# Identity products where TensorE waits, and a reordered router and transition, in a two-block model kernel

## Chip, cores and metric

The kernel runs on one NeuronCore of a Trainium2 chip. The metric is the device time of one execution in microseconds (us); before the change the median of three runs is 1951.22 us (1948.08 to 1958.10).

## What is computed

Two transformer blocks over 256 tokens of width 1024, in float32. The first mixes an mLSTM and a sparse attention under a modulation computed from `c`, and ends in a mixture of 32 experts; the second has two layers of attention, a recurrent branch and a feed-forward part. What the change touches, cut from the reference:

```python
mod = jnp.dot(jax.nn.silu(c), w_ada[l]) + b_ada[l]            # 1024 x 6144, in six parts
sh1, sc1, gt1, sh2, sc2, gt2 = [m[:, None, :] for m in jnp.split(mod, 6, axis=-1)]
h = rmsnorm(x, g_pre_mix[l]) * (1.0 + sc1) + sh1
...
h2 = rmsnorm(x, g_pre_ffn[l]) * (1.0 + sc2) + sh2
logits = jnp.dot(xf, w_router) + b_router                     # 32 experts
vals, idx = lax.top_k(logits, 4)
gate = jax.nn.softmax(vals, axis=-1)
...                                                           # each picked (token, expert) pair is evaluated
up = jnp.dot(xb, w_up[eb]) + b_up[eb]
glu, lin = jnp.split(up, 2, axis=-1)
act = jnp.minimum(glu, 7.) * jax.nn.sigmoid(1.702 * jnp.minimum(glu, 7.)) * (jnp.clip(lin, -7., 7.) + 1.0)
y = jnp.dot(act, w_down[eb]) + b_down[eb]
...
x = x + gt2 * rmsnorm(y2, g_post_ffn[l])                      # the hand-over to the second block
```

## The kernel before

The program is written by hand: one instruction stream for each engine, ordered by semaphores. Each engine works strictly in the order of its stream; TensorE's weight loads may run ahead of its products. Eight PSUM banks `pb[0..7]` of 128 x 512 float32 are assigned by hand.

*Modulation.* The first third of `w_ada`, as far as shift and scale of the first mix need it, comes in eight row slabs of 1 MB. `modulation(k)` (L1130, products at L1135) multiplies slab k with a column of `silu(c)`, four products of 512 columns into four strips of bank 6. After slab 6 two transposes turn the parameter rows (L1175, L1176); after slab 7 VectorE copies the bank (L809), `first_columns` (L1143) turns the row into columns, VectorE makes shift and scale (L814, L815) and h, one chunk at a time (L817). Then come the gate rows (`rows`, L1199: h against 32 gate columns), the flips of the attention bias (L1209, products with a flipped identity into banks 5, 6, 7, 3), a ScalarE and VectorE chain over the gates (L605 to L848), and the column units of `w_in` (L1191), which load slab by slab as earlier slabs are used up.

*Router.* The last output slab's columns are gained and turned (L1451) and `route` (L1459) adds up the logits in bank 7. VectorE makes X1 and later the top four of each token (L1042 to L1059), ScalarE its squares (L754) and the scaled rows h2 (L760). TensorE turns X1 into columns (L1488), then waits for `logits_ready` and makes the places of the picked pairs (L1493 to L1497: counts with the strict lower triangle `before` and with ones, for two token tiles). VectorE turns places into a selection (L1068 to L1071), TensorE gathers the rows of the first expert (`gather`, L1574), ScalarE copies them (L768), TensorE turns them (`turn_rows`, L1581, into bank 0) and ScalarE makes scaled columns of them (`expert_columns`, L567).

*Experts.* `tensor_pass` runs 34 passes of 64 rows: `up` (bias products L1603, then eight weight chunks L1612), `gather` of the next pass, `scatter` of the last pass (L1591, into banks 4 to 7), transposes (L1618, L1624), `down` (L1633). Pass 0 stands outside the loop and has some router work between its halves (`halfway`). Each expert's 12 slabs of 1 MB come as six double slabs through three double places, the anteroom; GpSimd copies them into the ring (L1553) when the slab's place is used up (`expert_used`), and SyncE issues the next double slab into the freed place (`sync_experts`, L1536 and L1540). The first three of expert 1 wait for h2 and the turned X1.

*Transition.* When the last scatter is done (`acc_done`), ScalarE squares the four result banks 4 to 7 (L2147) and loads the square root's table (L2148); VectorE scales the banks by `gt2` (L2322); TensorE sums the eight squared chunks over partitions (L1864); ScalarE takes the root (L2144), VectorE its reciprocal (L2324), the scaled parts (L2331) and the new x (L2328); ScalarE's scaled x (L2154) feeds the second block's first products (L1900). GpSimd's loads of the second block wait for the first square.

## Time and profile before

| | |
|---|---|
| median of 3 runs | 1951.22 us (1948.08 to 1958.10) |
| profiled execution | 1952.78 us, its span 1951.0 us |
| mean granted TensorE clock | 0.985 |
| TensorE busy | 1896.1 us, 97% of the span |
| GpSimd, VectorE, ScalarE busy | 706.7, 610.5, 410.1 us |
| chain that ended last | TensorE 84%, DMA 8%, VectorE 3% |
| DMA | 553.49 MB, mean 284 GB/s |

The profile is of one execution. Busy times are of instructions, not of waits; PE is TensorE, PEld its weight loads, DVE VectorE, ACT ScalarE, POOL GpSimd, SP SyncE.
### The profile page before, as it was taken

What the parts mean: (1) busy time and instruction counts of PE and PEld (TensorE: products, weight loads), DVE (VectorE), ACT (ScalarE), POOL (GpSimd) and SP (SyncE); (2) the same over time, 40 slices, a digit from 0 to 9 for tenths busy, and PEclk for the clock granted to TensorE, in tenths of its full rate; (3) what the DMA queues carried; (4) which work ended last, traced back from release to release, by engine and by line L of the source; (5) the groups of instructions that cost most, each with busy time, mean ns of one, the idle gap of its engine ahead of it and who ended that gap; (6) DMA issues with size and microseconds to landing.
All of it is one profiled execution on the core that took longest, in us unless ns stands there. A gap on an engine that the chain in (4) does not pass through costs nothing.

```text
span 1951.0 us, 25907 instructions
## 1 busy us (share of the span) xinstructions
PE 1896.1 (97%) x9600; PEld 1148.8 (59%) x9601; DVE 610.5 (31%) x1304; ACT 410.1 (21%) x981; POOL 706.7 (36%) x406
## 2 busy tenths in 40 slices
PE   7999999999999999999999998999999999999999
PEld 4886733333333333333333335877888888788887
DVE  1756422322332232223331333664010126521000
ACT  2134322212221222212211222351000003500000
POOL 0000057777777777777767772000000000000000
PEclk8999989999999999999999999999999999999999
DMA  9873889999999999999999999243434652344330
GB/s 353 269 251 120 314 335 425 427 427 424 429 426 388 427 426 425 428 425 426 427 395 428 426 425 324 92 130 129 130 105 110 185 190 85 114 140 146 96 104 22
DMA packets 194760, 553.49 MB, mean 284 GB/s; under 512 B 13387, under 2 KB 151006, under 8 KB 160910
## 3 DMA queue, kind: packets, MB, share of 16 engines
q1 hardware_dynamic: 189872, 549.45, 73.0%
q10 hardware_dynamic: 4270, 1.98, 0.4%
q0 software_dynamic: 560, 1.25, 0.3%
q8 instruction: 41, 0.67, 0.1%
q14 instruction: 17, 0.14, 0.0%
HBM read 551.59 MB, written 1.06 MB: 283 GB/s over the span
## 4 chain that ended last, share of the span: by engine, by line
PE 84%; DMA 8%; DVE 3%; issue 2%; POOL 2%; ACT 1%; SPq 0%; POOLq 0%; ACTq 0%; DVEq 0%
PE bank L1612 19%; PE bank L1885 18%; PE bank L1633 10%; PE bank L2118 8%; DMA ring_and_columns<-in_w_up_dram 7%; PE bank L1890 4%; PE bank L1191 3%; PE bank L1591 3%; PE bank L1574 3%; PE bank L1900 2%; PE bank L1199 2%; PE bank L1472 2%; POOL ring_and_columns L1553 2%; PE bank L2004 1%; PE bank L1603 1%
## 5 line engine op out<-in xcount | busy, mean ns | idle before, releaser
L1553 POOL COPY ring_and_columns<-ring_and_columns 128x2048 f32<-128x2048 f32 x248 | 463.1, 1898 | 244.3 <-PE bank L1612 107.2
L1612 PE MATMUL bank<-ring_and_columns,cst 128*64 128x512 f32 x2176 | 480.3, 597 | 8.2 <-POOL ring_and_columns L1553 8.2
L1612 PEld LDWEIGHTS bank<-ring_and_columns,cst 128*64 128x64 f32 x2176 | 151.7, 137 | 334.4 <-issue 289.5
L1885 PE MATMUL bank<-ring_and_columns 128*128 128x272 f32 (+1 forms) x1536 | 342.7, 386 | 0.0
L1885 PEld LDWEIGHTS bank<-ring_and_columns 128*128 128x128 f32 x1536 | 291.8, 190 | 49.9
L1553 POOL COPY ring_and_columns<-anteroom_last 128x2048 f32<-128x2048 f32 x124 | 231.5, 1897 | 68.7 <-DMA anteroom_last<-in_w_up_dram 30.2
L1633 PE MATMUL bank<-ring_and_columns,pass_work 128*64 128x512 f32 x1088 | 242.5, 598 | 5.4 <-DVE pass_work L1735 5.4
L1633 PEld LDWEIGHTS bank<-ring_and_columns,pass_work 128*64 128x64 f32 x1088 | 77.9, 137 | 148.2 <-issue 144.0
L2118 PE MATMUL bank<-ffn_act,ring_and_columns 128*128 128x272 f32 (+1 forms) x704 | 157.1, 386 | 0.0
L2118 PEld LDWEIGHTS bank<-ffn_act,ring_and_columns 128*128 128x128 f32 x704 | 133.7, 190 | 22.8
L1726 DVE TENSOR_SCALAR pass_work<-bank 128x512 f32<-128x512 f32 x34 | 23.5, 692 | 338.7 <-PE bank L1612 338.7
L1686 ACT ACTIVATE pass_work<-pass_work 128x512 f32<-128x512 f32 x34 | 21.4, 630 | 470.8 <-DVE pass_work L1726 470.8
L567 ACT ACTIVATE cst<-bank,expert_affine_by_pair 128x64 f32<-128x64 f32 x280 | 86.9, 417 | 88.2 <-PE bank L1581 88.2
L1711 DVE COPY hot<-cst 64x64 f32 x34 | 31.8, 936 | 231.0 <-PE bank L1603 231.0
L2548 DVE TENSOR_TENSOR probs<-bank,probs 128x272 f32<-128x272 f32 (+1 forms) x40 | 15.4, 427 | 251.5 <-ACT probs L2304 251.5
L1890 PE MATMUL bank<-ring_and_columns 128*128 128x256 f32 x384 | 85.5, 381 | 0.0
L1890 PEld LDWEIGHTS bank<-ring_and_columns 128*128 128x128 f32 x384 | 72.2, 190 | 11.5 <-issue 2.0
L1191 PE MATMUL bank<-ring_and_columns 128*128 128x256 f32 x320 | 70.6, 380 | 0.0
L2304 ACT ACTIVATE probs<-bank 128x272 f32<-128x272 f32 (+1 forms) x40 | 13.4, 388 | 269.6 <-PE bank L1885 269.6
L1591 PEld LDWEIGHTS bank<-cst,pass_work 64*128 64x128 f32 x544 | 49.7, 186 | 32.9 <-issue 26.8
L1574 PE MATMUL bank<-h_rows_sb,psel 128*64 128x512 f32 x280 | 67.6, 604 | 1.1 <-DVE psel L1071 1.1
L1591 PE MATMUL bank<-cst,pass_work 64*128 64x256 f32 x544 | 67.9, 389 | 0.7 <-ACT pass_work L1693 0.7
(506 smaller groups left out, 1718.3 us busy)
## 6 DMA issues: line engine op xcount, KB each, us to landing
ring_and_columns<-in_w_up_dram SPq DMA_DIRECT2D x97, 2048.0 KB, 10.6
ring_and_columns<-in_w_down_dram SPq DMA_DIRECT2D x33, 2048.0 KB, 10.6
anteroom_last<-in_w_up_dram SPq DMA_DIRECT2D x31, 2048.0 KB, 10.5
anteroom_last<-in_w_down_dram SPq DMA_DIRECT2D x31, 2048.0 KB, 10.7
ring_and_columns<-in_w_gu_dram SPq DMA_DIRECT2D x44, 1024.0 KB, 5.4
ring_and_columns<-in_w_in_dram SPq DMA_DIRECT2D x33, 1024.0 KB, 10.4
ring_and_columns<-in_w_down_dram SPq DMA_DIRECT2D x32, 704.0 KB, 6.1
ring_and_columns<-in_w_ada_dram SPq DMA_DIRECT2D x8, 2048.0 KB, 12.3
```

The lines of the kernel that those rows point to most:

```text
L567: ins = act.activation(xe[:, k, :], turned[:, k % (WIDE // P), k // (WIDE // P), :], ACT.Identity, bias=PAB[:, 0, k:k + 1], scale=PAB[:, 1 ...
L1191: ins = mm(dst, w(k), hv[:, k, :], start=(k == 0), stop=(k == CHUNKS - 1))
L1199: ins = mm(dst, hv[:, k, P * t:P * t + P], w(k), start=(k == 0), stop=(k == CHUNKS - 1))
L1472: ins = mm(y_bank(j, t)[:, y_at(j, t)], yv[:, k, P * t:P * t + P], w[:, k, :], start=(k == 0), stop=(k == CHUNKS - 1))
L1553: pool.tensor_copy(ring[:, k, :], anteroom(j % ANTE)[:, SLOT * half:SLOT * half + SLOT]).then_inc(ante_copied, 1)
L1574: ins = mm(bankG[CAP * g:CAP * g + CAP, 0:WIDE], psel[:, t, :], h2[:, t, WIDE * g:WIDE * g + WIDE], start=(t == 0), stop=(t == 1))
L1591: ins = mm(pb[4 + (WIDE // P * g + k) // 2][:, S * (k % 2):S * (k % 2) + S], ye[r, P * k:P * k + P], pgt[r, :], start=False, stop=False, s ...
L1612: ins = mm(bank[CAP * g:CAP * g + CAP, 0:WIDE], xe[:, k, :], ring[:, k, a:a + WIDE], start=False, stop=(k == CHUNKS - 1))
L1633: ins = mm(bankY[CAP * g:CAP * g + CAP, 0:WIDE], rows_, w[:, WIDE * g:WIDE * g + WIDE], start=(k == 0), stop=(k == CHUNKS - 1))
L1885: ins = mm(bank[:, 0:columns], w[:, k, P * m:P * m + P], src[:, k, 0:columns], start=(k == 0), stop=(k == CHUNKS - 1))
L1890: ins = mm(pb[bank][:, a:a + 256], hT[:, k, P * t:P * t + P], w[:, k, :], start=(k == 0), stop=(k == CHUNKS - 1))
L2118: ins = mm(pb[DOWN_BANKS[l][m]][:, 0:n], w[:, k, :], FA[:, kk, 0:n], start=(kk == 0), stop=(kk == NF - 1))
```

## The change

A helper `keep_busy(bank, n)` issues n products of the identity with the 256 constant columns that begin with the identity, into a bank that is unused there. It is called in the modulation (three ahead of slabs 5 and 6, two ahead of slab 7, two behind it, two behind the column products) and in the router (two ahead of the transposes of X1, two ahead of the wait for the logits, two behind the placement). The placement products become three with wider operands. VectorE's subtraction for the gates' exponential moves behind the mask that TensorE waits for. The first pass's turned rows go to bank 2 instead of bank 0, and `up` waits for its columns behind the bias products (pass 0) or behind the first half of them (later passes). In the transition the last scatter signals twice, the squares run in the order of banks 4, 6, 5, 7, VectorE adds the two halves of each squared bank so that TensorE sums four chunks instead of eight, and the scaling by `gt2` is merged into the scaling by the reciprocal.

```diff
-        def expert_columns(act):
-            turned = pb[0][:, 0:WIDE].rearrange("p (c g n) -> p c g n", c=WIDE // P, g=GROUPS)
+        def expert_columns(act, bank):
+            turned = bank[:, 0:WIDE].rearrange("p (c g n) -> p c g n", c=WIDE // P, g=GROUPS)
...
-            tt(RW[:, 3, :, :], LG[:], spread_last(V8[:, :, 0], E), ALU.subtract).then_inc(s["logit_exp_in"], 1)
             tt(RW[:, 0, :, :], LG[:], v4, ALU.is_gt)
...
             dve.sem_inc(s["logits_ready"], 1)
+            tt(RW[:, 3, :, :], LG[:], spread_last(V8[:, :, 0], E), ALU.subtract).then_inc(s["logit_exp_in"], 1)
...
+            def keep_busy(bank, n):
+                both = cst[:, cat["ident"][0]:cat["ident"][0] + S]
+                for _ in range(n):
+                    mm(bank[:, 0:S], ident, both, start=True, stop=True)
...
+            pe.wait_ge(s["trel_copied"], 1)
             for k in range(FIRST_CHUNKS, CHUNKS - 1):
+                if k >= 5:
+                    keep_busy(pb[7], 3)
                 modulation(k)
...
+            keep_busy(pb[7], 2)
             modulation(CHUNKS - 1)
+            keep_busy(pb[7], 2)
             pe.wait_ge(s["const_ready"], 7)
             pe.wait_ge(s["params_ready"], 1)
             first_columns()
+            keep_busy(pb[7], 2)
...
             route(3).then_inc(s["routed"], 1)
+            keep_busy(pb[3], 2)
             for b in range(4):
...
+            keep_busy(pb[3], 2)
             pe.wait_ge(s["logits_ready"], 1)
-            m0, m1 = RW[:, 5, 0, :], RW[:, 5, 1, :]
-            mm(pb[7][:, 0:E], C["before"], m0, start=True, stop=True)
-            mm(pb[7][:, E:2 * E], ones[:], m0, start=True, stop=False)
-            mm(pb[7][:, E:2 * E], C["before"], m1, start=False, stop=True)
-            mm(pb[7][:, 2 * E:3 * E], ones[:], m0, start=True, stop=False)
-            mm(pb[7][:, 2 * E:3 * E], ones[:], m1, start=False, stop=True).then_inc(s["placed"], 1)
+            both = RW[:, 5, :, :]
+            mm(pb[7][:, 0:2 * E], C["before"], both, start=True, stop=False, skip_group_check=True)
+            mm(pb[7][:, 2 * E:3 * E], ones[:], both[:, 1, :], start=False, stop=False, skip_group_check=True)
+            mm(pb[7][:, E:3 * E], ones[:], both[:, 0:1, :].broadcast_to([P, TT, E]), start=False, stop=True, skip_group_check=True)\
+                .then_inc(s["placed"], 1)
+            keep_busy(pb[3], 2)
...
-            def scatter(i, done):
+            def scatter(i, done, by_banks=False):
...
+                    if by_banks and k == 1:
+                        ins.then_inc(done, 1)
                 ins.then_inc(done, 1)
...
                 pe.wait_ge(q["u_free"], i + 1)
-                pe.wait_ge(q["x_rows"], i + 1)
                 pe.sem_inc(item_begun, 1)
                 for b, bank in ((1, bankU1), (0, bankU0)):
+                    if b == 0 and not halfway:
+                        pe.wait_ge(q["x_rows"], i + 1)
...
                 ins.then_inc(q["bias_used"], 1)
+                if halfway:
+                    pe.wait_ge(q["x_rows"], i + 1)
...
-            turn_rows(0)
+            turn_rows(0, bankY)
...
-            scatter(count, q["acc_done"])
+            scatter(count, q["acc_done"], by_banks=True)
...
+        BANK_ORDER = (0, 2, 1, 3)
...
-            for k in range(CHUNKS):
-                pe.wait_ge(*at("m_y", k // 2 + 1))
-                ins = mm(pb[0][:, 0:S], ones[:], sq[:, k, 0:S], start=(k == 0), stop=(k == CHUNKS - 1))
+            for n, b in enumerate(BANK_ORDER):
+                pe.wait_ge(*at("m_sq", n + 1))
+                ins = mm(pb[0][:, 0:S], ones[:], sq[:, 2 * b, 0:S], start=(n == 0), stop=(n == 3))
...
-            pool.wait_ge(*at("m_y", 1))
+            pool.wait_ge(*at("m_y", 3))
...
-            for b in range(4):
+            for n, b in enumerate(BANK_ORDER):
+                if n == 2:
+                    act.wait_ge(q1["acc_done"], 2)
                 act.activation(sqv[:, 2 * b:2 * b + 2, :], pb[4 + b][:].rearrange("p (k n) -> p k n", k=2), ACT.Square).then_inc(t2["m_y"], 1)
...
-            for k in range(CHUNKS):
-                dve.wait_ge(*at("m_y", k // 2 + 1))
-                ts(hv[:, k, :], pb[4 + k // 2][:, S * (k % 2):S * (k % 2) + S], gt2[:, k:k + 1], None, ALU.mult)
+            for n, b in enumerate(BANK_ORDER):
+                dve.wait_ge(*at("m_y", n + 1))
+                tt(sqv[:, 2 * b, :], sqv[:, 2 * b, :], sqv[:, 2 * b + 1, :], ALU.add).then_inc(t2["m_sq"], 1)
...
-                tt(hv[:, k, :], hv[:, k, :], rstd[:, 0:S], ALU.mult).then_inc(t2["m_part"], 1)
+                y = pb[4 + k // 2][:, S * (k % 2):S * (k % 2) + S]
+                stt(hv[:, k, :], y, gt2[:, k:k + 1], rstd[:, 0:S], ALU.mult, ALU.mult).then_inc(t2["m_part"], 1)
```

## Rows read from the trace of the kernel before

**Rows 1.** Chain of work that ended last, inside the experts: start us, us, what

```profile
483.87 10.70 DMA ring_and_columns<-in_w_up_dram
```

**Rows 2.** Busy time by stage: engines' busy us (instructions), granted clock, DMA share, GB/s

```profile
282.00:288.00 6.00, 6.00 (x34) 1.77 (x32) 0.57 (x1) 1.88 (x2) 5.63 (x4) 1.00 0.49 146
288.00:294.00 6.00, 6.00 (x32) 2.00 (x30) 2.18 (x2) 0.00 (x0) 5.73 (x4) 1.00 1.01 430
```

**Rows 3.** Timeline of GpSimd: start us, us, line, form, count [idle before, releaser]

```profile
280.23 3.73 POOL L1553 COPY ring_and_columns<-ring_and_columns 128x2048 f32<-128x2048 f32 x2 [7.90 <-PE bank L1633]
```

**Rows 4.** Timeline of TensorE in the modulation and the first units

```profile
25.59 1.06 PE L1135 MATMUL bank<-ring_and_columns,silu_c 128*32 128x512 f32 x8 [1.50 <-DMA ring_and_columns<-in_w_ada_dram]
...
28.23 1.93 PE L1135 MATMUL bank<-ring_and_columns,silu_c 128*32 128x512 f32 x8 [1.13 <-DMA ring_and_columns<-in_w_ada_dram]
31.07 1.84 PE L1143 MATMUL bank<-share,ring_and_columns 128*128 128x4 f32 x8 [0.91 <-DVE ring_and_columns L809]
34.02 7.00 PE L1199 MATMUL bank<-w_gate_rows,ring_and_columns 128*128 128x32 f32 x32 [1.11 <-DVE ring_and_columns L817]
...
40.84 5.34 PE L1209 MATMUL bank<-conv_out,cst 128*128 128x256 f32 x16
...
55.32 0.22 PE L1238 MATMUL bank<-cst,gate_work 4*128 4x4 f32 x1 [1.79 <-DVE max_rows L848]
```

**Rows 5.** Busy time by stage in the modulation, and at 130

```profile
24.00:27.00 3.00, 1.50 (x14) 0.43 (x10) 0.00 (x0) 0.00 (x0) 0.00 (x0) 1.00 1.02 406
...
36.00:39.00 3.00, 3.00 (x16) 3.00 (x15) 0.14 (x1) 0.00 (x0) 0.00 (x0) 0.50 1.13 348
...
45.00:48.00 3.00, 3.00 (x18) 2.51 (x17) 0.00 (x0) 1.78 (x4) 0.00 (x0) 1.00 1.06 368
...
130.00:133.00 3.00, 3.00 (x16) 2.68 (x17) 2.86 (x5) 0.00 (x0) 0.00 (x0) 0.50 1.07 389
```

**Rows 6.** Timeline of TensorE: column units, and products of few columns

```profile
77.36 14.06 PE L1191 MATMUL bank<-ring_and_columns 128*128 128x256 f32 x64
...
126.58 0.95 PE L1151 MATMUL bank<-ones,ring_and_columns 128*128 128x1 f32 x8
...
128.51 2.76 PE L1262 MATMUL bank<-k_cmp,q_nsa 64*128 64x15 f32 x32
```

**Rows 7.** Timeline of the router: mask, placement, gather, column activations, bias products

```profile
237.36 0.22 DVE L1048 TENSOR_TENSOR router_work<-logits,top 128x64 f32<-128x64 f32 x1
...
239.45 0.41 PE L1493 MATMUL bank<-router_work,cst 128*128 128x32 f32 x2 [0.92 <-DVEq L1060]
...
240.36 0.39 PE L1497 MATMUL bank<-router_work,ones 128*128 128x32 f32 x2
...
241.84 3.42 PE L1574 MATMUL bank<-h_rows_sb,psel 128*64 128x512 f32 x8 [1.09 <-DVE psel L1071]
...
246.74 2.48 ACT L567 ACTIVATE cst<-bank,expert_affine_by_pair 128x64 f32<-128x64 f32 x8 [0.84 <-PE bank L1581]
...
249.47 1.98 PE L1603 MATMUL bank<-b_up_sb,hot 32*64 32x512 f32 x8 [2.64 <-ACT cst L567]
```

**Rows 8.** Timeline of TensorE: gather and bias products of later passes

```profile
268.12 1.89 PE L1574 MATMUL bank<-h_rows_sb,psel 128*64 128x512 f32 x8
...
285.12 1.09 PE L1603 MATMUL bank<-b_up_sb,hot 32*64 32x512 f32 x8
```

**Rows 9.** Timeline of the transition: scatter, squares, sums, table load, second block's first products

```profile
1194.32 2.00 PE L1591 MATMUL bank<-cst,pass_work 64*128 64x256 f32 x16 [0.69 <-ACT pass_work L1693]
1196.36 2.06 ACT L2147 ACTIVATE ring_and_columns<-bank 128x512 f32<-128x512 f32 x4 [2.10 <-PE bank L1591]
1197.01 3.72 PE L1864 MATMUL bank<-ring_and_columns,ones 128*128 128x256 f32 x16 [0.70 <-ACT ring_and_columns L2147]
...
1198.44 1.28 ACT L2148 ACT_TABLE_LOAD   x1
...
1204.86 16.52 PE L1900 MATMUL bank<-ring_and_columns 128*128 128x272 f32 x64 [4.13 <-ACT ring_and_columns L2154]
```

10 lines of the change are left out of this document (5 added, 5 removed).

## The prediction

> **What bounds the kernel now.** I read the chain of work that ended last first: TensorE carries most of it, and the only long stretches that it does not carry are two spells inside the experts, in which the transfer of each weight slab ends last [rows 1]. The pieces there are one double slab each, 10.70 us from issue to landing, one behind the other. So a time saved ahead of the experts is worth something only if the weight stream moves with it. The busy times by stage answer that: between 282 and 288 the DMA engines are busy for 0.49 of the time and from 288 on for all of it [rows 2]. What held them is the copy on GpSimd that empties the anteroom, and that copy waited 7.90 us for expert 0's down products on TensorE [rows 3]. The stream's unbroken run therefore starts when TensorE lets it, and a shift of TensorE before 280 shifts the stream, both DMA-bound spells and the end by the same amount. The second block follows the experts with TensorE in the chain, so a shift of the hand-over passes through too. Three stretches are touched: 22 to 56 (modulation), 231 to 252 (router), 1194 to 1205 (transition).
>
> Next I read the granted clock beside TensorE's work. It is 1.00 at 24 to 27, 0.50 at 36 to 39 and 1.00 again at 45 to 48 [rows 5]: the lower of its two levels, 1.2 GHz, holds through the modulation's last product, the column products, the gate rows and most of the bias flips. Before it fell TensorE had waited 1.50 us for one slab [rows 4].
>
> **The change part by part.** A filler is one product of the identity with 256 columns. It leaves two matmul records; 64 records of that form took 14.06 us at the higher level [rows 6], so 0.22 each, 0.44 us a filler, and 0.88 at the lower level.
>
> *Modulation.* Eight fillers go ahead of slabs 5, 6 and 7: 3.5 us. The waits for slabs 6 and 7 (1.50 and 1.13 [rows 4]) cover 2.6 of it; the slabs come by DMA and are not moved. I charge 0.2 to the last slab; if nothing else is hidden it is 0.9. The two fillers ahead of the column products and the two behind them lie in waits of 0.91 and 1.11 for DVE [rows 4] and just fit at 0.88. The new wait for the copied bias row is over by then and queues nothing. If the higher level holds, the last modulation product takes 1.06 instead of 1.93 (the slab before against this one [rows 4]) and the column products, eight records, 0.95 instead of 1.84 (eight records of one column at the higher level [rows 6]): the gate rows start 0.9 + 0.9 - 0.2 = 1.6 us earlier. The gate rows themselves are 32 records in 7.00 us [rows 4]; at 0.12 a record they would be 3.8, so 3.2 less. The flips after them, 16 records, took 5.34 [rows 4], of which 0.2 run into what follows, and would be 3.5, so 1.7 less. Ends: -1.6 (the clock falls again at once and both run as before) and -6.5.
>
> Which end? TensorE was busy for 3.00 of 3.00 us at 130 to 133 and its clock stood at 0.50 [rows 5]; what it had done before the fall were products of one column and of 15 columns [rows 6]. Being busy is not enough, and the gate rows are 32 columns each, for 4 us or more, with no filler among them. I expect the clock to fall once during them and to come back in the flips, as it did before [rows 5]. DVE also feeds the first 16 of the gate rows one chunk at a time. I take -3.5, a little under the middle.
>
> The Trainium skill speaks for the other end. TensorE: Matmul & The Clock Gate, under "Part 1: The HAM clock gate", says that the clock is set by how busy the engine has been and falls after idleness; by that alone the fillers would hold it through the gate rows, and the sum would be the first rival's. The row of 130 to 133 shows a busy engine at the lower level [rows 5], so I do not follow it there.
>
> What is late next: after the flips ScalarE and DVE take 9.1 us to the gate's row maxima, and TensorE waits 1.79 us for them behind its first column unit [rows 4]. All of that hangs on the flips and moves with them; the column unit may lose up to 1.8 us to a lower clock at no cost.
>
> *Router.* Five placement products become three with more columns: the first and the last start 0.91 apart [rows 7], 0.23 a product, so 0.45 less, and DVE's subtraction (0.22 [rows 7], partly overlapped) moved behind the mask takes up to 0.2 off the chain before them: -0.6 together; at worst -0.4. The subtraction's reader, ScalarE's exponential, is not due until ScalarE has turned out the row columns. The gather behind took 3.42 us at the lower level [rows 7]; at the higher it takes 1.72 to 1.89 [rows 8]: between 0 and -1.7. The two fillers right ahead of it must fit between the placement and the selection, a wait of 1.09 [rows 7]: 0.88 at the higher level does, 1.76 at the lower does not and costs 0.7. Between them the placement products are again narrow and short, with waits on both sides, so I expect the lower level about as often as not in part of the gather: -0.8.
>
> The bias products of expert 0 stood behind the eight activations that make its columns (2.48 us) and took 1.98 more [rows 7]. They now run before that wait, in a bank that the turned rows no longer occupy. At the lower level they need 1.98 and fit under the 2.48 of ScalarE; at the higher 1.09 [rows 8]. So 1.98 and the 0.2 of their own start leave the path: -2.1. The first weight products still begin at the lower level, as before; I give that nothing. In the loop of later passes the same wait moves by four products, where the columns are long ready: nothing. Router: -0.6 - 0.8 - 2.1 = -3.5; ends -1.8 (0.7 of filler, 0.4 placement, 2.1) and -4.4.
>
> *Transition.* Before: scatter ends, four squares (0.61 to the first), eight sums over partitions on TensorE, 3.72 to 1200.73, root, reciprocal [rows 9]. After: banks 4 and 6 are done at half of the scatter's 2.00 us, so two squares run under its second half; the last square ends some 1.0 us earlier, and ScalarE's table load of 1.28, which starts when the squares are done [rows 9], too. DVE adds the halves and four sums remain on TensorE, the last behind the last square by an addition of 256 columns on DVE and two records, an estimate of 0.9 us; the table load and the small root after it (1.28 + 0.2) end later than that and now set the root. It starts at 1197.4 + 1.5 = 1198.9 instead of just behind 1200.73: -1.8. The scaling by the gain moves into the eight products behind the reciprocal, which read PSUM; in the same order and number, perhaps 0.1 dearer on the two that the path sees: ends -1.4 and -1.9. GpSimd's loads wait for the third square, which now comes when the first did. The idle stretch before the second block stays about 4.1 us [rows 9], so it starts at the lower level as before.
>
> **Sum.** -3.5 - 3.5 - 1.8 = -8.8. The profiled execution took 1952.78 (span 1951.0, 1.8 around it): 1944.0 by it. It lies 1.6 over the median of the runs, 1951.22; from that, 1942.4. I forecast 1942.5. Own range: all low ends (-1.6, -1.8, -1.4) -4.8, all high ends (-6.5, -4.4, -1.9) -12.8, so 1938.4 to 1946.4.
>
> **The rivals.**
> - *The clock holds throughout*: every stretch runs at the higher level, -12.8, 1938.4. For it: the fillers fill just the waits before the fall. Against it: the row of 130 to 133 [rows 5]. The Trainium skill's rule above gives this case. Chance 0.26.
> - *The fillers do not touch the clock*: only the reordering counts, and the fillers hide: modulation 0 to +0.9, placement -0.6, a filler at the lower level ahead of the gather +0.7, bias products -2.1, transition -1.8: -3.4, 1947.8. That is the change not doing what it says. Against it: at 45 to 48 the level came back behind 16 records of the fillers' very form [rows 4, 5]. Chance 0.11.
> - *The stream swallows the router's part*: expert 1's first slabs are issued before the router's end and do not move with it; if they, not TensorE, set the unbroken run, the 3.5 is lost: 1945.9. For it: the chain's DMA spells [rows 1]. Against it: rows 2 and 3. Chance 0.07.
> - *Slower: fillers at the lower level stand in the way.* If the clock is still low when slab 5 is due, a filler costs 0.88 and TensorE, which works in order, has all of this ahead of the modulation's columns: ten fillers 8.8, three slab products of 1.93, the column products 1.84 and two short transposes (0.6), 17.0 us from 23.0 (slab 6's product at 25.59 less its wait and slab 5's like product [rows 4]), so to 40.0 instead of 32.9: +7.1; the last two fillers hide behind DVE. With the filler ahead of the gather (+0.7) and the parts that need no clock (-2.1 - 0.6 - 1.8) that is +3.3, 1954.5. It decides the sign from the point where the clock is at the lower level at 22 us and stays there for all ten. Against it: the level at 24 to 27 is 1.00 [rows 5], and fillers are the work that raised it at 45. Chance 0.06.
>
> **How the numbers follow.** Forecast 0.50, rivals 0.26, 0.11, 0.07, 0.06. Predicted is the forecast's 1942.5. The range for 8 in 10 takes in the forecast's own range, the first rival and the stream's, and 2 us on either side for the runs of before, which lie 1948.08 to 1958.10: 1936.5 to 1948.5; what stays out is the slower rival and the rest of that scatter. A measurement of this kernel can tell about 0.5% from no change, 9.8 us, so the line is 1941.5. The first rival lies under it (0.26) and about a third of the forecast's chance (0.16): faster 0.42. Slower by 9.8 needs two mishaps beyond the last rival: 0.02. Same: 0.56.
>
> **What would show it.** In the profile after: the granted clock at 27 to 32 should be 1.00 and the gate rows should start near 32.4; a fall within the gate rows confirms my middle, none the first rival. The first weight products of expert 0 should start near 244.4 (now 251.4), and the bias products should stand ahead of the column activations' end. The gap in the DMA before the unbroken run should keep its length; if it vanishes the stream has swallowed the gain. In the transition the root should follow directly on the table load and the small root behind it. I am wrong if the modulation's end or the gather gets later, or if the experts get longer.

## The result and the profile after

The changed kernel takes 1942.07 us (median of 12 runs, 1937.50 to 1948.18) against 1951.44 (12 runs) of the kernel before: 0.9947 of its time, 95% interval 0.9938 to 0.9956 (the two medians alone give 0.9952). The profiled execution took 1940.99, its span 1939.1, so 11.9 less than the span before (1951.0) and some 2.5 more than the medians differ. The forecast of 1942.5 was met almost to the microsecond, but not by the terms that made it up. The spans between a few landmarks of the two traces show it:

| stretch, from one landmark to the next | before | after | difference | forecast |
|---|---|---|---|---|
| start to the small gate products on TensorE | 55.32 | 56.50 | +1.2 | -3.5 |
| to ScalarE's first square of X1 (233.05, 232.03): no line changed | 177.73 | 175.53 | -2.2 | 0 |
| router, to expert 0's first weight products (251.38, 246.20) | 18.33 | 14.17 | -4.2 | -3.5 |
| expert 0, to the second product of the up projection (286.14, 275.79) | 34.76 | 29.59 | -5.2 | 0 |
| the other experts, to the last scatter (1194.32, 1184.05) | 908.18 | 908.26 | +0.1 | 0 |
| transition, to the second block's first products (1204.86, 1192.90) | 10.54 | 8.85 | -1.7 | -1.8 |
| second block, to the end of the span | 746.1 | 746.2 | +0.1 | 0 |

The modulation comes first. This is TensorE's timeline after the change (start us, us, line, form, count, and in brackets the idle time before with what ended it); L1143 are the products of the identity.

```profile
25.59 1.06 PE L1135 MATMUL bank<-ring_and_columns,silu_c 128*32 128x512 f32 x8
26.59 1.56 PE L1143 MATMUL bank<-cst 128*128 128x256 f32 x6
28.08 1.06 PE L1135 MATMUL bank<-ring_and_columns,silu_c 128*32 128x512 f32 x8
...
29.52 1.13 PE L1143 MATMUL bank<-cst 128*128 128x256 f32 x4
30.59 1.06 PE L1135 MATMUL bank<-ring_and_columns,silu_c 128*32 128x512 f32 x8
...
32.55 1.03 PE L1149 MATMUL bank<-share,ring_and_columns 128*128 128x4 f32 x8
...
35.07 5.98 PE L1211 MATMUL bank<-w_gate_rows,ring_and_columns 128*128 128x32 f32 x32 [0.52 <-DMA w_gate_rows<-in_w_in_dram]
40.86 6.50 PE L1221 MATMUL bank<-conv_out,cst 128*128 128x256 f32 x16
...
56.50 0.22 PE L1250 MATMUL bank<-cst,gate_work 4*128 4x4 f32 x1 [1.79 <-DVE max_rows L848]
```

Against [rows 4] the waits for slabs are gone and the last slab's product and the column products are as fast as forecast (1.06, 1.03). But everything stands later: the last slab's product begins at 30.59 instead of 28.23, the gate rows at 35.07 instead of 34.02, and their last wait is now one for their own weights, which had not been in the way before. Some 1.2 us of this seem to belong to this execution and not to the change: its slabs came late from the first on (first product at 11.40, before at 10.20), while four of the five other kernels with these products and unmoved transfers have that product at 10.39 to 10.65. The clock, in the busy times by stage (engines' busy us, then granted clock, DMA share, GB/s), after the change:

```profile
32.00:35.00 3.00, 2.55 (x16) 1.85 (x14) 1.62 (x6) 0.00 (x0) 0.00 (x0) 1.00 1.15 310
35.00:38.00 3.00, 2.93 (x19) 2.96 (x19) 1.80 (x6) 0.00 (x0) 0.00 (x0) 0.72 1.16 327
38.00:41.00 3.00, 3.00 (x16) 3.00 (x15) 0.00 (x0) 0.00 (x0) 0.00 (x0) 0.50 1.08 375
...
246.00:262.00 16.00, 15.80 (x74) 5.40 (x76) 5.04 (x12) 3.77 (x8) 11.14 (x6) 1.00 1.00 425
262.00:275.00 13.00, 12.91 (x66) 6.50 (x66) 2.83 (x6) 3.85 (x12) 8.86 (x5) 1.00 1.04 420
273.00:276.00 3.00, 3.00 (x20) 0.80 (x18) 0.00 (x0) 1.09 (x2) 3.00 (x3) 1.00 0.99 314
```

The higher level (2.4 GHz) now holds to 35, as forecast, and falls within the gate rows, as forecast; what was gained there the later start takes back, and from the gate rows' start to the flips' end it is 12.29 instead of 12.16. From 246 to 276 the clock is at the higher level throughout. Before the change it was not; the same view of the kernel before:

```profile
250.00:262.00 12.00, 12.00 (x48) 3.44 (x42) 0.64 (x5) 1.40 (x4) 6.50 (x4) 0.76 0.62 238
262.00:275.00 13.00, 13.00 (x58) 6.37 (x55) 7.09 (x9) 2.44 (x3) 8.44 (x5) 0.92 0.98 415
275.00:288.00 13.00, 13.00 (x58) 4.72 (x58) 1.68 (x4) 4.63 (x11) 7.41 (x4) 0.82 0.69 263
```

That is two spells at the lower level (1.2 GHz), one at expert 0's beginning and one around its down products. The timeline of TensorE before shows what they cost:

```profile
251.38 9.26 PE L1612 MATMUL bank<-ring_and_columns,cst 128*64 128x512 f32 x32
...
269.94 4.37 PE L1657 MATMUL bank<-gates_t_sb,b_down_sb 32*128 32x256 f32 x16
...
276.58 8.62 PE L1633 MATMUL bank<-ring_and_columns,pass_work 128*64 128x512 f32 x32
...
286.14 13.95 PE L1612 MATMUL bank<-ring_and_columns,cst 128*64 128x512 f32 x64
```

and router and expert 0 after the change (TensorE, and ScalarE's column activations) what became of them:

```profile
238.29 0.43 PE L1507 MATMUL bank<-router_work,cst 128*128 128x64 f32 x2 [1.42 <-DVEq L1059]
...
240.26 1.94 PE L1588 MATMUL bank<-h_rows_sb,psel 128*64 128x512 f32 x8 [0.18 <-DVE psel L1071]
...
243.67 2.48 ACT L567 ACTIVATE cst<-bank,expert_affine_by_pair 128x64 f32<-128x64 f32 x8 [0.83 <-PE bank L1595]
...
243.69 1.09 PE L1620 MATMUL bank<-b_up_sb,hot 32*64 32x512 f32 x8
246.20 7.09 PE L1631 MATMUL bank<-ring_and_columns,cst 128*64 128x512 f32 x32 [1.42 <-ACT cst L567]
...
262.58 3.72 PE L1676 MATMUL bank<-gates_t_sb,b_down_sb 32*128 32x256 f32 x16
...
267.76 7.09 PE L1652 MATMUL bank<-ring_and_columns,pass_work 128*64 128x512 f32 x32
```

The bias products lie under the column activations, the gather takes 1.94 instead of 3.42 [rows 7], and the weight products wait only for the activations. Of expert 0's 5.2 us, 2.2 come from its first half (9.26 to 7.09) and 3.0 from the stretch between the rows of 269.94 and 286.14 (16.20, now 13.21 from 262.58 to 275.79).

The copy on GpSimd that held the weight stream for 7.90 [rows 3] waited half as long:

```profile
269.87 3.73 POOL L1567 COPY ring_and_columns<-ring_and_columns 128x2048 f32<-128x2048 f32 x2 [3.91 <-PE bank L1652]
```

and the transition, in order of time:

```profile
1184.05 2.00 PE L1605 MATMUL bank<-cst,pass_work 64*128 64x256 f32 x16 [0.69 <-ACT pass_work L1712]
1185.23 2.06 ACT L2169 ACTIVATE ring_and_columns<-bank 128x512 f32<-128x512 f32 x4 [1.23 <-PE bank L1605]
1186.57 1.99 PE L1884 MATMUL bank<-ring_and_columns,ones 128*128 128x256 f32 x8 [0.53 <-DVE ring_and_columns L2344]
1187.31 1.28 ACT L2170 ACT_TABLE_LOAD   x1
1188.72 0.46 ACT L2164 ACTIVATE rstd<-bank,eps 128x256 f32<-128x256 f32 x1
1192.90 16.59 PE L1920 MATMUL bank<-ring_and_columns 128*128 128x272 f32 x64 [4.33 <-ACT ring_and_columns L2176]
```

The first square starts 1.18 behind the scatter's start (before 2.04, [rows 9]), the table load follows the last square, and the root follows the load and the small root behind it.

### The profile page after: what moved, and what is told of

Read it like the earlier page. It is cut to its first block, busy times and chain, and to the rows that moved or that the text cites. A ratio compares the mean times of both kernels' runs of the same rounds, so it can differ in the third digit from the quotient of the medians.

```text
span 1939.1 us, 25920 instructions
## 1 busy us (share of the span) xinstructions
PE 1889.5 (97%) x9624; PEld 1146.6 (59%) x9625; DVE 611.9 (32%) x1300; ACT 410.0 (21%) x981; POOL 706.7 (36%) x406
## 3 DMA queue, kind: packets, MB, share of 16 engines
q10 hardware_dynamic: 4270, 1.98, 0.4%
HBM read 551.59 MB, written 1.06 MB: 285 GB/s over the span
## 4 chain that ended last, share of the span: by engine, by line
PE 64%; DMA 23%; issue 4%; POOL 4%; DVE 2%; ACT 1%; ACTq 0%; POOLq 0%; SPq 0%; DVEq 0%
DMA ring_and_columns<-in_w_up_dram 21%; PE bank L1905 18%; PE bank L1631 9%; PE bank L2138 8%; PE bank L1652 5%; PE bank L1910 4%; POOL ring_and_columns L1567 4%; PE bank L1203 3%; PE bank L1920 2%; PE bank L1211 2%; PE bank L2024 1%; PE bank L1484 1%; PE bank L1605 1%; PE bank L1588 1%; PE bank L2020 1%
## 5 line engine op out<-in xcount | busy, mean ns | idle before, releaser
L1741 DVE TENSOR_SCALAR cst<-cst,place,gate_of 128x128 f32<-128x128 f32 x68 | 66.4, 1016 | 12.0 <-issue 12.0
## 6 DMA issues: line engine op xcount, KB each, us to landing
anteroom_last<-in_w_up_dram SPq DMA_DIRECT2D x31, 2048.0 KB, 10.5
anteroom_last<-in_w_down_dram SPq DMA_DIRECT2D x31, 2048.0 KB, 10.7
```

The source lines that it names most:

```text
L1741: ins = ts(pg[:, t, :], C["iota"], pmx[:, t, bass.ds(j, 1)], gx[:, t, bass.ds(j, 1)], ALU.is_equal, ALU.mult)
```

## The experiments

Each kernel was run 5 to 12 times and one of these executions profiled. The table holds the time as a ratio to runs of the kernel before on the same chip, and landmarks (us) of the one profile. Where they disagree the ratio decides on the time. In the kernels without the early weights the first square of X1 lies between 228.75 and 233.83, with no order that follows the edits ahead of it; a stretch is therefore compared by its own length.

| kernel | ratio (95%) | flips end | first square of X1 | router stretch | expert 0 stretch | second block starts | second block takes |
|---|---|---|---|---|---|---|---|
| before | 1 | 46.18 | 233.05 | 18.33 | 34.76 | 1204.86 | 746.1 |
| changed | 0.9947 (0.9938 to 0.9956) | 47.36 | 232.03 | 14.17 | 29.59 | 1192.90 | 746.2 |
| modulation alone | 1.0004 (0.9995 to 1.0014) | 45.71 | 230.37 | 18.52 | 31.55 | 1198.86 | 746.0 |
| router products alone | 1.0000 (0.9992 to 1.0009) | 47.77 | 232.44 | 15.96 | 31.23 | 1198.58 | 751.9 |
| router order alone | 0.9990 (0.9978 to 1.0002) | 47.27 | 230.25 | 16.31 | 34.72 | 1199.94 | 746.2 |
| transition alone | 0.9984 (0.9972 to 0.9995) | 46.28 | 233.15 | 18.24 | 34.85 | 1203.10 | 747.1 |
| router, both parts | 0.9980 (0.9971 to 0.9990) | 46.94 | 233.83 | 14.18 | 29.59 | 1196.28 | 752.3 |
| all but modulation | 0.9949 (0.9937 to 0.9962) | 47.06 | 230.00 | 14.17 | 30.97 | 1191.98 | 746.2 |
| all but router products | 0.9971 (0.9961 to 0.9982) | 45.65 | 232.52 | 15.49 | 31.49 | 1196.53 | 746.3 |
| early weights | 1.0018 (1.0005 to 1.0030) | 60.70 | 245.35 | 14.18 | 29.59 | 1206.77 | 746.1 |
| early weights, fewer products | 1.0007 (0.9993 to 1.0021) | 57.24 | 240.26 | 14.18 | 29.59 | 1202.08 | 746.1 |
| late by four | 0.9969 (0.9957 to 0.9982) | 45.65 | 230.35 | 14.16 | 29.60 | 1192.50 | 752.2 |
| late by eight | 0.9966 (0.9953 to 0.9979) | 45.90 | 228.84 | 14.17 | 30.99 | 1194.35 | 746.5 |
| products among gate rows | 0.9961 (0.9948 to 0.9974) | 44.05 | 228.75 | 14.15 | 31.04 | 1191.25 | 746.3 |

The router stretch runs from the first square of X1 to expert 0's first weight products, expert 0's from there to the second product of the up projection. The last five kernels are variants of the changed one.

### The parts alone

**Modulation alone.** The kernel before with the helper and the modulation's calls only; the call for two stands ahead of slab 7, behind it, and behind the column products.

```diff
+            pe.wait_ge(s["trel_copied"], 1)
             for k in range(FIRST_CHUNKS, CHUNKS - 1):
+                if k >= 5:
+                    keep_busy(pb[7], 3)
                 modulation(k)
...
+            keep_busy(pb[7], 2)
```

> Only the twelve fillers of the modulation are added to the kernel before. Theory one (the gate rows' weights land at about 34 to 35 us whatever TensorE does, and the clock falls inside the gate rows): the gate rows start no earlier than in the kernel before, the flips end within 1.5 us of where they ended, and the time is within 2 us of the kernel before. Theory two (the prediction's term): -3.5 us, with gate rows starting near 32.4 and an end of the flips some 3.5 earlier. Theory three (fillers ahead of the slabs queue in TensorE's way): 1 to 4 us slower.

Measured: no difference, 1.0004, theory one. Its profiled execution was the lowest of its runs (1946.60 against a median of 1953.54), so its landmarks speak for the stage alone: gate rows at 35.09, as in the changed kernel, but flips that end 0.5 earlier than before and not 1.2 later. TensorE's timeline, and below it the loading of instructions among the DMA queues from 26 to 30 us (transfers, MB, share of 16 engines):

```profile
29.63 1.06 PE L1135 MATMUL bank<-ring_and_columns,silu_c 128*32 128x512 f32 x8 [0.23 <-DMA ring_and_columns<-in_w_ada_dram]
...
35.09 4.53 PE L1211 MATMUL bank<-w_gate_rows,ring_and_columns 128*128 128x32 f32 x32 [1.50 <-DMA w_gate_rows<-in_w_in_dram]
```

```profile
q8 instruction: 1, 0.02, 1.7%
```

Here the last slab itself comes late: its product waits for it and still begins at 29.63. Ten kernels have their first slab's product at 10.2 to 10.7. In the six of them without the modulation's products the last slab's product begins at 28.23 to 28.76, in the four with them at 29.53 to 29.63. The transfer of instructions (16 KB, 1.1 us) starts at 38.0 to 38.6 in the six and at 27.1 to 27.2, ahead of the last slab's landing, in the four. That the twelve more products in TensorE's stream bring it forward, and that it holds the slab up, was not tested by itself.

**Router products alone.** One call ahead of the transposes of X1, one ahead of the wait for the logits, one behind the placement.

```diff
+            keep_busy(pb[3], 2)
```

> Only the six fillers of the router are added; placement, bias products and transition stay as before. Theory one (the fillers keep the granted clock at the higher level through gather and expert 0): -3 to -7 us, the gather in about 1.9 instead of 3.4, expert 0's products up to the end of its down products without a half-clock spell. Theory two (the prediction's weighing: the clock is lost as often as not, and expert 0's own products gain nothing): about -0.5. Theory three: the fillers only queue, 0 to +1.5.

Measured: the gather took 1.94, the router stretch became 2.4 us shorter and expert 0's 3.5. That is theory one in the stage; in the time it fell, which did not move: the second block began 6.3 earlier and took 5.8 longer. The last experiments take that up.

**Router order alone.** The three placement products, the moved subtraction, the turned rows in bank 2 and the moved wait, without products of the identity.

```diff
+            expert_columns(act, pb[2]).then_inc(q1["x_rows"], 1)
...
+                    if b == 0 and not halfway:
+                        pe.wait_ge(q["x_rows"], i + 1)
```

> Placement in three products, the moved subtraction, the turned rows in bank 2 and the bias products ahead of their wait; no filler anywhere, transition as before. Theory one: -2.7 us (0.6 placement and mask, 2.1 bias products), the clock still at the lower level in the gather and at the start of expert 0. Theory two (the bias products between gather and expert 0 keep the clock up by themselves): -5 to -7.

Measured: the router stretch became 2.0 shorter. The gather still took 3.68, the bias products 1.98 at 244.10, under the activations, and both of expert 0's spells stayed (9.22 for its first half, 8.57 for the down products). The time agrees with a small gain and with none.

**Transition alone.** The two signals of the scatter, the order of banks, the four sums and the merged scaling.

```diff
+            for n, b in enumerate(BANK_ORDER):
+                dve.wait_ge(*at("m_y", n + 1))
+                tt(sqv[:, 2 * b, :], sqv[:, 2 * b, :], sqv[:, 2 * b + 1, :], ALU.add).then_inc(t2["m_sq"], 1)
```

> Only the transition is changed. Theory one: -1.8 us, from the last scatter's end to the second block's first product 6.7 instead of 8.5. Theory two (the idle stretch before the second block is as long and the clock is low at its start either way, or the dearer products that read PSUM give it back): within 0.5 of the kernel before.

Measured: 8.86 from the scatter to the second block, as in the changed kernel, 1.7 less than before; 0.9984 agrees within its interval.

The four ratios add up to 0.9978, the changed kernel has 0.9947: 6 us more than the parts, with an uncertainty of some 4.5 (all five intervals). The four profiled spans do nearly add up (-6.1, -0.5, -4.9 and -0.8 against -11.9), but two of them come from executions 6.9 and 2.5 below the median of their runs.

### What each part is worth within the whole

**All but modulation**: the changed kernel without the modulation's calls of the helper and the wait ahead of them.

> The change without its products of the identity in the modulation; router and transition as changed. Theory one, the products of the modulation are worth nothing (in the changed kernel they delayed the last slab's product from 28.23 to 30.59 and the gate rows from 34.02 to 35.07): the gate rows start at 34.0 to 34.5 again and the ratio to the kernel before stays at 0.994 to 0.996, the changed kernel's own. Theory two, the modulation earns a part of the gain after all, by where the later spells at 1.2 GHz then fall: 0.997 to 0.999, near what the three single parts add up to, and the clock of 228 to 291 is no longer 1.00 throughout.

Measured: 0.9949, the changed kernel's own time. TensorE's timeline without these products:

```profile
28.59 1.93 PE L1135 MATMUL bank<-ring_and_columns,silu_c 128*32 128x512 f32 x8 [1.15 <-DMA ring_and_columns<-in_w_ada_dram]
...
34.37 7.00 PE L1205 MATMUL bank<-w_gate_rows,ring_and_columns 128*128 128x32 f32 x32 [1.11 <-DVE ring_and_columns L817]
```

The last slab's product waits again and runs at the lower level, and yet the gate rows begin 0.7 earlier than with the products. Theory one held in the time and for the gate rows; the flips ended at 47.06.

**Router, both parts**: the kernel before with the products and the new order.

> The router's two parts together, the products of the identity and the new order, with the modulation and the transition as before. Theory one, the parts add: the single runs gave 1.0000 and 0.9990, so 0.999 (some 1950). Theory two, they need each other: the products hold the clock only as far as the next hole, and it is the new order that takes the hole of the column activations out of the way; the clock is then 1.00 from 228 to 291, expert 0's second product of the up projection starts near 276 to 277 instead of 279.6 and 281.3 in the single runs and 286.1 before, and the ratio is 0.995 to 0.997.

Measured: 0.9980, between the two. In the router stretch the parts simply add: 2.4 and 2.0 alone, 4.2 together. In expert 0 they do not: 3.5 and 0 alone, 5.2 together, with the clock at 1.00 from 228 to 281, as theory two has it. The second block again took 6 longer and hid most of it.

**All but router products**: the changed kernel without the router's three calls of the helper.

> The change without its products of the identity in the router; modulation, new order and transition as changed. Theory one, by the stage: with the new order alone expert 0's second product of the up projection started at 281.28, with the whole change at 275.79, so some 5 us are lost here: 1946 to 1948, ratio 0.997 to 0.998. Theory two, the new order alone keeps the clock once the program before it is placed as in the changed kernel, and the products are worth nothing: 0.994 to 0.996.

Measured: 0.9971, theory one. Timeline of TensorE, and the clock by stage:

```profile
240.75 2.88 PE L1585 MATMUL bank<-h_rows_sb,psel 128*64 128x512 f32 x8 [1.09 <-DVE psel L1071]
...
248.01 8.97 PE L1628 MATMUL bank<-ring_and_columns,cst 128*64 128x512 f32 x32 [0.49 <-ACT cst L567]
```

```profile
228.00:246.00 18.00, 14.27 (x80) 10.59 (x82) 12.32 (x60) 12.36 (x29) 0.00 (x0) 0.78 0.68 249
```

Without the products the mean granted clock of the router is 0.78, the gather takes 2.88 and expert 0's first half 8.97. Within the whole they are worth 0.0024 of the time, 4.7 us, with an uncertainty of some 2.7 (both intervals); in the profiles 3.7.

### Why the modulation gave nothing

**Early weights**: the changed kernel with the transfers of the gate rows' weights right behind the meta tokens, ahead of the parameter rows.

```diff
             act.dma_start(metain[:], meta_tokens_2).then_inc(s["x_in"], 16)
+            act.dma_start(wga[:, :, 0:8], w_in[0, :, C_I:C_I + 8].rearrange("(k p) n -> p k n", p=P)).then_inc(s["gate_in"], 16)
+            act.dma_start(wga[:, :, 8:32], w_in[0, :, C_GA:C_GA + 24].rearrange("(k p) n -> p k n", p=P)).then_inc(s["gate_in"], 16)
```

> The change, with the two transfers of the gate rows' weights issued some 4 us earlier on ScalarE's queue, right behind the meta tokens. Theory one, the gate rows of the changed kernel wait 0.52 for these weights and otherwise for the eight modulated tiles of h that VectorE writes from 34.13 to 36.80: they start at 34.5 instead of 35.07, and end no earlier than 0.5, so the ratio moves by under 0.0005 from the changed kernel's. Theory two, the arrival is what hid the forecast gain of the modulation: gate rows and flips then run in part at 2.4 GHz and the flips end at 44 or earlier instead of 47.38, 1.5 to 3 us less in all.

Measured: 1.0018, 13.8 us worse than the changed kernel, which neither theory had. ScalarE's queue of issues, in its timeline, names the cause:

```profile
2.73 0.60 ACTq L502 DMA_DIRECT2D w_gate_rows<-in_w_in_dram  x1
3.36 18.93 ACTq L509 DMA_DIRECT2D param_rows<-in_b_ada_dram  x1
```

The issue moved by 10.5 us and not by 4 (12.72 to 2.25). The next one on that queue, 24 KB of parameter rows, took 18.93, ScalarE did no work until it and five short ones were out, and TensorE stood for 22.14 until `silu(c)` was there. The whole program moved by 13.3 (flips end 60.70, 47.36). Measured from the column products, the gate rows begin 0.4 earlier than in the changed kernel (2.14 behind them against 2.52) and the flips end 1.4 earlier (13.39 against 14.81). Against the modulation alone, all but router products and the two late kernels, which have the same modulation (3.49 to 3.59, and 14.09 to 14.19), the gate rows begin 1.4 earlier and the flips end 0.7 to 0.8 earlier. As far as this disturbed run can tell, the weights' landing is worth that much and does not account for the whole of the lost 3.5. One more thing shows: TensorE is so late that the transfer of instructions starts at 43.3, and the last slab lands 22.6 behind its issue at 5.93, as early as in the kernels without the modulation's products.

**The same with fewer products**: two instead of three ahead of slabs 5 and 6, none ahead of slab 7.

```diff
                 if k >= 5:
-                    keep_busy(pb[7], 3)
+                    keep_busy(pb[7], 2)
...
-            keep_busy(pb[7], 2)
             modulation(CHUNKS - 1)
```

> As the run before it with the early weights, and fewer products of the identity in the modulation: four instead of six ahead of slabs 5 and 6, none ahead of the last. Theory one, in the changed kernel six of them (1.56 us) and a slab's product (1.06) fill the 2.6 us between two slabs' landings, so that the late start and the turned parameters never drain and the last slab's product came at 30.59; with fewer it comes at 28.5 to 29.5, the gate rows start at 33 to 33.5 and the flips end at 45 to 46, 1 to 2 us less than in the changed kernel. Theory two, the fewer products let the clock fall before the gate rows: columns and gate rows at 1.2 GHz as before the change, flips ending at 46 to 47, no difference.

Measured: the same blocked queue (18.99), so all slabs had long landed and the times of theory one can't be seen in it. It is inconclusive. The flips end 13.24 behind the column products, as in the run before.

**Products among the gate rows**: the changed kernel with one product of the identity ahead of every second of the first eight gate products.

```diff
+                    if first and k % 2 == 1:
+                        keep_busy(pb[7], 1)
                     ins = mm(dst, hv[:, k, P * t:P * t + P], w(k), start=(k == 0), stop=(k == CHUNKS - 1))
```

> The change, with four more products of the identity between the first eight products of the gate rows, where TensorE waits for the modulated tiles of h (some 2 us of work, against 1.3 to 1.5 of waiting). Theory one, it is the gate rows' products on 32 columns that let the clock fall in the modulation: with the others between them the gate rows and flips run at 2.4 GHz, the flips end at 43 to 45 instead of 47.38, and the kernel gains 2 to 4: ratio 0.9925 to 0.9935. Theory two, the clock falls a few us later instead, in the flips, or what follows waits for its slabs: the flips end at 46 to 48 and the ratio stays at 0.994 to 0.996.

Measured: theory one in the stage. Timeline of TensorE and clock by stage:

```profile
38.42 2.09 PE L1213 MATMUL bank<-w_gate_rows,ring_and_columns 128*128 128x32 f32 x18
40.35 3.70 PE L1223 MATMUL bank<-conv_out,cst 128*128 128x256 f32 x16
...
53.18 0.22 PE L1252 MATMUL bank<-cst,gate_work 4*128 4x4 f32 x1 [1.79 <-DVE max_rows L848]
```

```profile
37.00:40.00 3.00, 3.00 (x25) 2.90 (x25) 0.00 (x0) 0.00 (x0) 0.00 (x0) 1.00 1.13 349
40.00:43.00 3.00, 3.00 (x17) 2.71 (x17) 0.00 (x0) 1.68 (x3) 0.00 (x0) 1.00 1.05 386
```

A gate-row record takes 0.12 at the higher level, as the prediction priced it, the flips 3.70 instead of 6.50, and the small gate products come at 53.18 instead of 56.50. All 3.3 us reach expert 0's first products (242.90 against 246.20). Part of the 3.3 is the changed kernel's late slabs: against the modulation alone, all but router products and the two late kernels (small gate products at 54.78 to 55.03) it is 1.6 to 1.9. In expert 0 the first half takes 8.53 instead of 7.09, a spell at the lower level that the changed kernel does not have, and 1.7 is left at the second block's start. Over the runs nothing is left: 0.9961 against 0.9947, with intervals that overlap. It is no better kernel.

### Why the parts do not add up

**Late by four and by eight**: the changed kernel with four, or eight, multiplications by one between root and reciprocal.

```diff
             dve.wait_ge(*at("m_root", 1))
+            for _ in range(4):
+                st(ts(rstd[:, 0:S], rstd[:, 0:S], 1.0, None, ALU.mult))
             st(dve.reciprocal(rstd[:, 0:S], rstd[:, 0:S]))
```

> The change, with four extra multiplications by one on VectorE in the transition, between the root and its reciprocal: a pure delay of the second block by an estimated 1.4 to 1.8, no work taken away or moved. Theory one, what follows does not depend on when it begins: the second block takes 746 again, 1943.5 to 1944, ratio 0.9955 to 0.996. Theory two, the second block's time depends on when it begins, through a spell at 1.2 GHz in its attention, as it took 751.9 and 752.3 in two of the runs before and 746 in the others: with its start near 1194.5 it may take 752, so 1949 to 1950, ratio 0.9985 to 0.999, a loss of 6 to 8 for a delay of 1.6.

> As the run before it with eight such multiplications, so a delay of 2.8 to 3.6. Theory one: twice the loss of the delay by four, 1945 to 1946. Theory two, the start of the block decides: at about 1196 it comes where the router's run had it (1196.28) and took 752.3, so 1951 to 1952, ratio near 1.000; or, if the disturbance comes and goes with the start, less time than with four multiplications although the delay is twice as long.

Measured: the transition grows by 1.5 with four (scatter to second block 10.36) and by 2.8 with eight (11.67). In the profiles the second block takes 752.2 with four and 746.5 with eight, so the longer delay costs less. Busy times by stage show where; each kernel's stretch begins 100 us into its second block. Changed kernel, late by four, late by eight, and router with both parts:

```profile
1292.90:1312.90 20.00, 18.54 (x93) 14.59 (x94) 8.01 (x25) 7.93 (x36) 0.00 (x0) 1.00 0.00 1
```

```profile
1292.50:1312.50 20.00, 20.00 (x82) 15.09 (x82) 5.56 (x28) 9.53 (x43) 0.00 (x0) 0.79 0.01 3
```

```profile
1294.35:1314.35 20.00, 18.54 (x94) 14.54 (x93) 8.01 (x27) 8.00 (x37) 0.00 (x0) 1.00 0.00 1
```

```profile
1296.28:1316.28 20.00, 20.00 (x81) 15.13 (x82) 5.59 (x27) 9.55 (x43) 0.00 (x0) 0.79 0.01 2
```

It is one spell at 1.2 GHz in the attention of the second block. The same twelve products of queries and keys take 1.18 in the changed kernel and 2.13 in the one with four; TensorE's timelines:

```profile
1290.20 1.18 PE L1998 MATMUL bank<-qk 64*128 64x128 f32 x12
```

```profile
1291.42 2.13 PE L1998 MATMUL bank<-qk 64*128 64x128 f32 x12
```

What TensorE did before is the same list of instructions in both. The spell is there in three of fourteen profiles (router products, router with both parts, four late) and costs 5.7 to 6.1. Over the runs four late costs 0.0022 (4.3 us) and eight late 0.0019 (3.7), each with an uncertainty of some 3: too wide to tell the delay of 1.5 from theory two's 6 to 8. The runs of the kernel with four lie between 1942.14 and 1950.70. Whether the spell is in some and not in others is not shown: only the profiled one can be looked into, and with the spell it lies in the middle (1946.51). So the spell is a candidate for what the single parts lack, and no more.

## Why the prediction was right, and where it was wrong

That the number was right is luck: two errors of size cancelled. In the changed kernel's profile the modulation gave +1.2 where I had -3.5 (in four other profiles with the same modulation -0.3 to -0.5), and expert 0 gave -5.2 where I had written "I give that nothing". A further -2.2 came where no line changed. The rest (router, transition, and what passes through) held.

**Router: right, by its own steps.** From ScalarE's first square to the placement 6.26 instead of 6.40: -0.14, the subtraction's "up to 0.2". From the first placement product to the gather 1.97 instead of 2.39: -0.42, forecast -0.45. Bias products off the path: the weight products begin 0.05 behind the activations instead of 2.16, so -2.1, as forecast. The gather -1.48, forecast -0.8: I had weighed the lower level as likely as not, and the products ahead of it settled it. That they did it is shown by the runs without them (2.88, 3.68) and with them (1.94, alone and in the whole). All eight kernels with both parts have a router stretch of 14.15 to 14.18.

**Expert 0: a term that was missing.** The step that failed is "the first weight products still begin at the lower level, as before". With the bias products at the higher level ahead of them, they did not, and the spell around the down products went too. The first half took 7.09 in five of the eight profiles that have both parts of the router and 8.5 in the other three; with one part or none it took 8.7 to 9.4. The spell around the down products was there before, with the router's order alone and with the transition alone (expert 0 stretch 34.7 to 34.9), and absent in every kernel with products of the identity, the modulation alone among them (31.55), although that one changes nothing near it. Why it went there is open.

**Modulation: the mis-sized term, and a step that was false.** I charged "0.2 to the last slab; if nothing else is hidden it is 0.9". Its product came 2.36 later, and its end, being faster, 1.5. Of the 2.36 some 1.2 is the late start of this execution's slabs (the last was issued at 6.16 and landed 23.3 later, before at 5.88 and 22.3). The other 1.1 is products of the identity that still stood ahead of the slab when it had landed: three of them take 1.49 up to what follows them, 0.25 a record and not 0.22, and the three ahead of slab 5 hid behind nothing, since TensorE came free for it at 24.10, just as it landed.

In the four kernels whose slabs started as before (modulation alone, all but router products, late by four, products among the gate rows) nothing was left standing ahead of the last slab: its product waited 0.23 to 1.07 for it, and yet began only at 29.53 to 29.63. So the step "the slabs come by DMA and are not moved" failed. In these four the last slab itself came some 1.1 later than without the products. The early loading of instructions goes with it: it is there in all four, and where TensorE came late (early weights) both were gone. But there the weights' transfers had moved as well, so this cause is likely and not shown.

Behind it stood the cap that I had not looked for, the landing of the gate rows' weights at 34.98 (issued at 13.22, 21.76 underway). The gate rows waited 0.52 for them here and 1.46 to 1.59 in the five other kernels with these products. In the trace of before these weights were issued at 12.06 and nobody waited for them. I had the gate rows at 32.4; they began at 35.03 to 35.30 in all six.

The clock fell once within the gate rows, as I took it. From the gate rows' start to the flips' end that gave nothing in the changed kernel's profile and 1.5 to 1.6 (10.57 to 10.62 instead of 12.16) in the modulation alone, all but router products and the two late kernels, where I had 1.9. What it would be worth to avoid the fall is shown by the products among the gate rows: 1.6 to 1.9 us against these four, 3.3 against the changed kernel. By my own sign, "I am wrong if the modulation's end or the gather gets later", this part was wrong in the changed kernel's profile. That the modulation's products give nothing to the kernel's time is shown twice: 1.0004 alone, and 0.9949 against 0.9947 without them; a gain or loss of up to some 3 us stays inside the intervals.

**Transition: right.** -1.7 for -1.8, in the profiles of the part alone and of the whole, by the steps named: the root follows the small root, and the scaling in eight products costs 0.88 for the first two.

**The stream.** I had written that the DMA's gap before the unbroken run should keep its length, and that if it vanished the stream would have swallowed the gain. It did vanish, from a share of 0.49 at 282 to 288 [rows 2] to 0.99 at 273 to 276, and nothing was swallowed: the other experts took 908.26 instead of 908.18. The gap goes with a slow expert 0: the copy waits 7.90 to 8.32 in the three kernels where that stretch takes 34.7 to 34.9, and 3.91 here. My reading of the gap was wrong, the claim it should test was right.

**The rivals.** The clock did not hold throughout (0.50 at 38 to 41), and it did not stay untouched (1.00 at 32 to 35, 246 to 276); fillers at the lower level did not stand in the way. Of the Trainium skill's rule (TensorE: Matmul & The Clock Gate, "Part 1: The HAM clock gate"), that the clock follows how busy the engine has been, the traces bear out one half: the router's products, put into waits, did hold it. For the other half the gate rows are a counterexample. TensorE was busy for 2.93 of 3.00 us at 35 to 38, and the clock fell to 0.72 and then 0.50; with four wide products among those of 32 columns, in the same place, it stayed at 1.00.

**What stays open.** Why the second block's spell comes. It was there with a delay of 1.5 and not with one of 2.8, but each kernel was profiled once, so it is not shown that the delays brought it and took it away; and its start alone does not decide it: 1192.50 has it and 1192.90 not, 1198.58 has it and 1198.86 not. And the 2.2 us between the modulation and the router, where no line changed, go with spells of the same kind that fell elsewhere (120 to 132 at a mean of 0.90 before and 0.99 after, 160 to 200 at 0.91 and 1.00, 218 to 232 at 0.88 and 1.00, but 132 to 140 at 0.73 and 0.58). From the small gate products to the first square of X1 the fourteen profiles have only three lengths, 173.8 to 173.9, 175.5 to 175.6 and 177.7, in no order that follows the edits; the first square itself moves by up to 5 between the kernels, and what decides it was not found.

## What to carry to other kernels

Products that keep the clock up pay where a long run of wide products follows the wait (the router: a gather and half an expert), and not where narrow products follow and the clock falls among them again (the modulation). Before filling a wait on TensorE, add up all that is to go into it and look for the next arrival that caps the gain; in this case a slab that came later than before, and behind it a transfer of 128 KB that nobody had waited for. Where spells at the lower clock move with every edit, judge an edit of 2 us by its own stretch of the trace and by taking it out of the whole, not by its time alone or by adding the times of the parts.

## What the runs showed of the hardware

An edit that moved 128 KB of transfers up by some 10 us cost 14: with two small transfers of narrow rows ahead of it the next issue on ScalarE's queue, 24 KB, lasted 18.93 instead of 0.44, and the engine stood still meanwhile. The Trainium skill (DMA: Bandwidth & Descriptors, "Issuing engines are not separate DMA queues") calls the time that a sequencer takes to initiate a transfer usually small against the transfer itself; here it was 18.93, and no landing of this transfer is recorded to set beside it. In the changed kernel too, where the two transfers come later, a later issue on that queue took 6.42, beside other work.

With twelve more products in TensorE's stream a load of 16 KB of instructions starts at 27.1 to 27.2 us instead of 38.0 to 38.6, and the last slab's product begins at 29.53 to 29.63 instead of 28.23 to 28.76 (four profiles and six, in which the slabs start alike).

One spell at the lower level in the second block, with the same instructions ahead of it, is there in the profile with a delay of 1.5 us and absent in those without one and with 2.8. It costs 6 us, four times the delay.
